# Two transformer blocks on one core: block 1's mixing stage put in another order, attention first, gates split around the state steps

## What is computed

```python
h = rms_norm(x, mix_norm)
p_rwkv, p_q, p_k, p_v, p_gate = split(h @ w_in)         # 3360, 768, 768, 768, 2048 columns
# branch a: RWKV-7
r, k, v, wd, ad, gd = split(p + (prev - p) * mu)        # prev: the token before
decay = exp(-exp(-softplus(-(w0 + tanh(wd) @ w2)) - 0.5)); a = sigmoid(a0 + ad @ a2); g = sigmoid(gd) @ g2
kk = k * k_k;  kk = kk / max(norm(kk over each head's 64), 1e-12)
k = k * (1 + (a - 1) * k_a)
wkv = scan over tokens of a 64x64 state for each of 16 heads
y_a = (groupnorm(wkv) * ln_w + ln_b + sum(r * k * r_k) * v) * g
# branch b: dilated attention, 3 groups of 4 heads (dilations 1, 4, 16), causal
q, k = rms_norm over each head's 64;  s = q k^T / 8 + mask;  softmax; o = p v
y_b = o * softmax over the 3 groups of each group's log-sum-exp
g_a, g_b = split(sigmoid(p_gate + b_gate))
x = x + (g_a * (y_a @ w_proj_rwkv) + g_b * (y_b @ w_proj_attn)) @ w_out
```

## Time and profile before

| | us |
|---|---|
| median of 3 runs | 3079.72 (3071.02 to 3081.1) |
| the profiled execution | 3080.11 |
| its span, first to last instruction | 3078.5 |
| PE busy | 2830.0 (92%) |
| DVE busy | 760.7 (25%) |
| ACT busy | 361.0 (12%) |
| the mixing stage of block 1 (PE's first product to its last) | 586.65 |

### The profile page before, as it was taken

The page is one execution under the profiler, slowest core; times in us unless marked ns, Lnnn a source line. Parts: engine busy times, 40 slices in busy tenths (PEclk is TensorE's granted clock), DMA queues, the critical chain, the costliest instruction groups (busy, mean ns, idle before and its releaser), DMA issues.

```text
span 3078.5 us, 70725 instructions
## 1 busy us (share of the span) xinstructions
PE 2830.0 (92%) x32566; PEld 2331.4 (76%) x32566; DVE 760.7 (25%) x1322; ACT 361.0 (12%) x807; POOL 9.4 (0%) x21
## 2 busy tenths in 40 slices
PE   7998968993989999998999899989999999999997
PEld 6776857872667766873776667747999999999995
DVE  0002247546177733332000233321000000000002
ACT  1001122213010012410000124101000000000000
POOL 0000000000000000000000000000000000000000
PEclk9999989896999999998999899989999999999999
DMA  4433320030333432332344323325999999999993
GB/s 189 163 151 150 125 96 3 4 111 21 123 124 147 164 147 89 137 137 100 123 163 165 139 96 117 129 100 212 375 398 369 376 403 371 377 391 373 377 387 124
DMA packets 54385, 596.12 MB, mean 194 GB/s; under 512 B 6128, under 2 KB 6512, under 8 KB 8672
## 3 DMA queue, kind: packets, MB, share of 16 engines
q1 hardware_dynamic: 52464, 587.71, 48.9%
q0 software_dynamic: 1776, 6.20, 0.6%
HBM read 592.83 MB, written 1.05 MB: 193 GB/s over the span
## 4 chain that ended last, share of the span: by engine, by line
PE 88%; DVE 6%; DMA 3%; ACT 1%; issue 1%; SPq 0%; DVEq 0%; ACTq 0%
PE bank L306 20%; PE bank L1994 18%; PE bank L397 15%; PE bank L2006 9%; PE bank L314 8%; PE bank L408 7%; DMA slot<-in_experts 2%; PE bank L791 2%; PE bank L2087 1%; PE bank L373 1%; PE bank L2039 1%; PE bank L1574 1%; DVE arena L1156 1%; PE bank L774 0%; PE bank L1462 0%
## 5 line engine op out<-in xcount | busy, mean ns | idle before, releaser
L1994 PE MATMUL bank<-arena,slot 128*64 128x96 f32 x14336 | 615.4, 246 | 8.1 <-issue 6.2
L1994 PEld LDWEIGHTS bank<-arena,slot 128*64 128x64 f32 x14336 | 601.3, 137 | 11.7 <-issue 11.3
L397 PE MATMUL bank<-h_cm,slot 128*128 128x256 f32 x2112 | 464.8, 381 | 3.9 <-DVE h_cm L349 2.8
L306 PE MATMUL bank<-h_cm,slot 128*128 128x256 f32 (+1 forms) x2064 | 456.2, 383 | 3.6 <-DVE h_cm L351 2.3
L397 PEld LDWEIGHTS bank<-h_cm,slot 128*128 128x128 f32 x2112 | 403.8, 191 | 72.5 <-issue 18.4
L306 PEld LDWEIGHTS bank<-h_cm,slot 128*128 128x128 f32 (+1 forms) x2064 | 394.2, 191 | 65.0 <-issue 9.7
L2006 PE MATMUL bank<-ff,slot 128*64 128x96 f32 x7168 | 319.9, 246 | 13.5 <-DMA slot<-in_experts 10.3
L2006 PEld LDWEIGHTS bank<-ff,slot 128*64 128x64 f32 x7168 | 306.3, 137 | 15.9 <-issue 15.0
L2154 DVE TENSOR_TENSOR ff<-ff,bank 128x192 f32<-128x192 f32 x112 | 39.7, 354 | 800.5 <-PE bank L1994 800.5
L408 PE MATMUL bank<-slot,ff 128*128 128x512 f32 x528 | 231.5, 592 | 0.0
L408 PEld LDWEIGHTS bank<-slot,ff 128*128 128x128 f32 x528 | 100.3, 190 | 113.5 <-issue 111.9
(11 more groups left out here) (358 smaller groups left out, 1678.0 us busy)
## 6 DMA issues: line engine op xcount, KB each, us to landing
slot<-in_experts SPq DMA_DIRECT2D x112, 2048.0 KB, 8.9
slot<-in_experts SPq DMA_DIRECT2D x112, 1024.0 KB, 9.2
slot<-in_ffn SPq DMA_DIRECT2D x22, 2048.0 KB, 9.1
slot<-in_ffn SPq DMA_DIRECT2D x22, 1024.0 KB, 4.9
slot<-in_dense SPq DMA_DIRECT2D x11, 2048.0 KB, 8.8
slot<-in_dqk SPq DMA_DIRECT2D x8, 2048.0 KB, 8.5
slot<-in_g SPq DMA_DIRECT2D x8, 2048.0 KB, 8.1
slot<-in_w_in_rkv SPq DMA_DIRECT2D x6, 2048.0 KB, 8.2
```

The source lines that it names most:

```text
L306: ins = pe.matmul(ps[0:m, j * S:(j + 1) * S], w[:, k * width + c0:k * width + c0 + m], rhs[:, k, :], start=k == 0, stop=k == ks - 1)
L397: ins = pe.matmul(bank[:, m * S:(m + 1) * S], slot[s][:, c0:c0 + P], h_cm[:, k, :], start=k == 0, stop=k == KD - 1)
L1994: ins = pe.matmul(bank[64 * c:64 * c + 64, m * PLACES:(m + 1) * PLACES], slot[s][:, c0:c0 + 64], QUEUE[:, e, k, :], start=k == 0, stop=k = ...
```

## The change

The stage's products are put in another order, and several small computations get another form:

1. PE begins with q and k (packed so that slab n holds the tiles of three products for each half `u` of the heads), then k of RWKV, and lays the steps of attention between the products of v, r, k and the small products (`pe_block1`, with `act_block1` and `dve_block1`).
2. Gate slabs 0 and 1 stand at the end of `pe_block1`, ahead of the chunks; slabs 2 and 3 stand between the state steps.
3. `head_sums` makes each head's sum into 32 rows of one bank (3 or 4 matmuls with 32 output columns in one bank), the root and the reciprocal are done there on 512 columns, and `head_spread` spreads the result with matmuls over 32 rows, one bank each. This replaces the wide form for `qks`, `kks` and `gnv`.
4. The softmax over the keys of all three groups of a head is done at once, with one maximum and one sum over the groups; the second softmax over the groups is gone.
5. The projection of y_b (`attn_branch`) stands beside the group norm's steps, and y_a and the merged sum are passed on in four parts (`y_a_ready`, `merged1`).
6. The small RWKV matrices are a slab of the stream in place of three loads at the start; at the start c_dilated (576 KB) is loaded in place of c_rwkv (320 KB), and POOL's queue loads c_rwkv when both halves' masks were used. c_always is 128 columns (64 KB) wider.

```diff
+        for name, n in (("w_in_a", 0), ("w_in_qk", 0), ("w_in_qk", 1), ("w_in_qk", 2), ("w_in_rkv", 2), ("w_in_rkv", 3),
+                        ("w_in_v0", 0), ("w_in_v1", 0), ("lora", 0), ("w_in_rkv", 0), ("w_in_rkv", 1), ("w_in_rkv", 4),
+                        ("w_in_rkv", 5), ("w_in_gates", 0), ("w_in_gates", 1), ("w_in_gates", 2), ("w_in_gates", 3),
+                        ("w_proj_attn", 0), ("w_proj_attn", 1), ("w_proj_rwkv", 0), ("w_proj_rwkv", 1), ("w_out", 0), ("w_out", 1)):
+            stream.append(((name, n), dram[name][n], dram[name].shape[2]))
...
+        def head_sums(pe, key, src, pairs):
+            ps = fill(pe, key, next_bank())
+            for q, n in enumerate(pairs):
+                ins = pe.matmul(ps[32 * q:32 * q + 32, :], headones[:, 48:80], src[:, n:n + 2, :], start=True, stop=True)
+            filled(ins, key)
+        def head_spread(pe, key, q, src):
+            rows = slice(32 * q, 32 * q + 32)
+            ps = fill(pe, key, next_bank())
+            filled(pe.matmul(ps[:, :], pick[rows, :], src[rows, :], start=True, stop=True), key)
...
+            for n in range(4):
+                qk(n)
+            qk_sums(0)
+            qk(4)
+            qk(5)
+            qk_sums(1)
+            rkv(2)
+            qk_spread(0)
+            rkv(3)
+            qk_spread(1)
+            scores(0)
+            product_tm(pe, ("va0", 0), next_bank(), w, 512, 0, 512, h_cm, KD, 0)
+            scores(1)
+            product_tm(pe, ("va0", 1), next_bank(), w, 512, 0, 512, h_cm, KD, 1)
...
+            head_sums(pe, ("kks", 0), TMP, range(0, 8, 2))
...
+            turned_probs(0)
+            lora("w", w)
...
+                head_spread(pe, ("kkb", b), b, KKI)
+            lora("a", w)
+            lora("g", w)
+            attn_out(0)
+            turned_probs(1)
+            rkv(0)
+            attn_out(1)
+            rkv(1)
+            rkv(4)
...
+            rkv(5)
+            pe_gate(pe, 0)
+            pe_gate(pe, 1)
...
+            states(1)
+            pe_gate(pe, 2)
+            states(2)
+            pe_gate(pe, 3)
+            states(3)
             pe.wait_ge(named("wkv_ready"), 1)
...
+            pe.wait_ge(named("centred_squared"), 4)
+            head_sums(pe, ("gnv", 0), CUM, range(0, 8, 2))
...
+            attn_branch(0)
+            pe.wait_ge(named("gn_inverse"), 1)
+            for b in range(4):
+                head_spread(pe, ("gnb", b), b, GNI)
+            attn_branch(1)
...
-            ch.step(nc.vector.reciprocal(CUM, CUM))
-            ch.step(nc.vector.tensor_tensor(TMP, TMP, CUM, ALU.mult))
-            ch.step(nc.vector.tensor_tensor(TMP, TMP, spread(col("ln_w", 0, 8), S), ALU.mult))
-            ch.step(nc.vector.tensor_tensor(TMP, TMP, spread(col("ln_b", 0, 8), S), ALU.add))
-            ch.step(nc.vector.tensor_tensor(TMP, TMP, BONUS, ALU.add))
-            nc.vector.tensor_tensor(K, TMP, G, ALU.mult).then_inc(named("y_a_ready"), 1)
...
-            pool.wait_ge(named("y_a_ready"), 1)
-            pool.dma_start(turn_consts[:, 0:3 * KEYS], dram["c_dilated"]).then_inc(named("masks_loaded"), 16)
+            pool.wait_ge(named("masks_used"), 1)
+            pool.dma_start(turn_consts[:, 0:CONSTANTS["rwkv"].shape[1]], dram["c_rwkv"]).then_inc(named("rwkv_consts"), 16)
...
-            sp.dma_start(arena[:, 20480:21504], dram["lora_wa"]).then_inc(named("lora_loaded"), 16)
-            sp.dma_start(arena[:, 18432:19456], dram["lora_g"]).then_inc(named("lora_loaded"), 16)
-            sp.dma_start(arena[0:32, 19456:20480], dram["lora_g2"]).then_inc(named("lora_loaded"), 16)
```

More of the change, by code:

```diff
@@ L120, in constants @@
     add("always", "headones", row // HD == col // HD)
+    add("always", "pick", row % 32 == 16 * (col // HD))
     half = 16
@@ new lines, in pe_block1 @@
+            lora("a", w)
+            lora("g", w)
+            released(("lora", 0), ("g", 3))
+            attn_out(0)
[4 more added lines that the diff above has]
+            rkv(4)
+            pe.wait_ge(named("rk_ready"), 1)
+            for b in range(4):
+                ps = fill(pe, ("bonus", b), next_bank())
+                filled(pe.matmul(ps[:, :], headones, TMP[:, 2 * b:2 * b + 2, :], start=True, stop=True), ("bonus", b))
+            rkv(5)
@@ new lines, in pe_block1, with act_gate, act_block1, keep_raw @@
+            pe_gate(pe, 0)
+            pe_gate(pe, 1)
+        def act_gate(act, tile):
+            dst = (gates_a, gates_b)[tile // 8]
+            ps = full(act, ("gate", tile))
+            for j in range(2):
+                ins = act.activation(dst[:, tile % 8 + j, :], ps[:, j * S:(j + 1) * S], ACT.Sigmoid,
+                                     bias=col("b_gate", tile + j))
+            free(ins, ("gate", tile))
+        def act_block1(act, ch):
+            def keep_raw(n):
+                key, parts = SHIFTS[n]
@@ L668, in act_rwkv_in @@
-            for tile in range(0, 16, 2):
-                if tile == 4:
-                    act_decays(act)
-                ps = full(act, ("gate", tile))
-                for j in range(2):
-                    ins = act.activation(gates[:, tile + j, :], ps[:, j * S:(j + 1) * S], ACT.Sigmoid,
-                                         bias=col("b_gate", tile + j))
-                free(ins, ("gate", tile))
-        def act_decays(act):
+                free(act.copy(raw[n % 2][0:m, 0:len(parts), 1:S + 1],
+                              ps[0:m, 0:len(parts) * S].rearrange("p (k s) -> p k s", s=S)), key)
@@ L693, in dve_rwkv_in, with dve_block1, shift @@
+            attn_out(0)
+            probs(1)
+            keep_raw(6)
+            keep_raw(7)
+            attn_out(1)
+            for n in range(8, 14):
+                keep_raw(n)
+            for tile in (0, 2, 4, 6):
+                act_gate(act, tile)
+        def dve_block1(dve, ch):
+            def shift(n):
+                key, parts = SHIFTS[n]
                 drained(dve, key)
@@ new lines, in turned_probs @@
+            def turned_probs(u):
+                for n in (1, 3):
+                    ps = full(dve, ("pt", u, n))
+                    free(nc.vector.tensor_copy(PT_FLAT[:, 512 * n:512 * n + 512], ps[:, :]), ("pt", u, n))
+            h_written(dve, ("norm", "mix"))
+            for i in range(2):
+                ch.add(nc.vector.memset(raw[i][:, :, 0:1], 0.0))
+            ch.fence()
+            dve.sem_inc(named("shift_zero"), 1)
+            shift(0)
+            shift(1)
+            qk_meansq(0)
@@ L867, in pe_rwkv_chunks, with states @@
                     drained(pe, ("QG", j, c))
[L868 removed]
+            def states(c):
                 pe.wait_ge(named("state_ready"), c)
```

677 lines of the change are left out of this document (355 added, 322 removed).

## The result

| | before | after |
|---|---|---|
| median, us | 3080.41 (3071.02 to 3084.22, 4 runs) | 2981.84 (2973.96 to 2984.4, 4 runs) |
| ratio after / before | | 0.968, 95% interval 0.9651 to 0.9709 |
| the profiled execution, its span | 3080.11, 3078.5 | 2980.48, 2978.7 |
| the mixing stage | 586.65 | 488.1 |
| from its end to the end of the program | 2228.2 | 2227.6 |

The forecast was 2982. The stage runs from 263.04 to 751.14 us. It gave 98.5 of the 99.8 us by which the span is shorter; the rest of the program before it and after it is 0.6 us shorter each.

What follows compares the result with a forecast made beforehand. The stage was taken as bound by the order of PE's work around DVE's chains. Terms 231.1 + 8.3 + 129.5 + 118.9 = 487.8 against 586.65, 98.9 less; 3080.1 - 98.9 + 1.0 = 2982.2, forecast 2982, 8-in-10 range 2968 to 3004.

Steps and rivals of the forecast that it cites:

- work in the block (with 2.0 for shape changes): Stage up to `tm`: products and small operations 225.8 us, plus 2.0 for some ten tile-shape changes at 0.2.
- Bound by the order of PE's work around DVE's chains: Mixing stage: PE stands still 107 of 586.65 us, nearly all behind DVE chains, while products needing none stand further down.
- a whole start: Tile-mode changes: if 0.9 us were lost at each of some twelve, the sum would be 9 us higher.
- Narrow matmuls side by side: `head_sums` and `head_spread`: neighbours overlap, 0.9 to 1.1 us per group; rival, one after another, 17 us more, chance 0.15.
- The 1.3 ahead of the second `qks`: In the block, PE waits 1.3 us for ACT's square of the last q/k product.
- the 1 us in hand ahead of the first spread: Half 0's `qk_inverse`, under the r/k/v product of 13.8 us, is done 1 us before PE wants it.
- The 2.0 us for the banks of g: Half 1's transpositions `pt` wait 2.0 us for g's four banks, which ACT reads only after its three exponentials.
- the 1.1 us for a bank behind y_a's parts: Behind the chunks, PE waits 1.1 us for a bank DVE frees after y_a's four parts, 10.6 us in all.
- the second rival: DVE or ACT late inside the new block: 2.5 us at each of five places, 12 us, 2994; chance 0.17.
- Gates between the state steps hide both waits: Behind the chunks, gate products of 27.6 us hide both waits between the three state steps.
- The reason for taking off 1.3 us: Chunks 130.8 us less about 1.3, since their first matmuls no longer follow a long stand: 129.5.
- The clock: Rival: lowered clock on 345 us of PE work outside the chunks takes part or all of the gain; chance 0.04.

Runs made afterwards that it cites:

- e4: Changed kernel with gate slab 1's two products in the first two turns of the chunk loop; median 2973.44 us, stage 490.2 us.
- e9: The kernel of e4 run once more with nothing edited; median 2969.97 us, stage 478.6 us.
- e2: Changed kernel with gate slabs 2 and 3 behind the third state step instead of between the steps; median 2978.46 us.
- e7: Kernel before, in its old order, with only kk, q and k given the narrow form (head_sums, head_spread); median 3047.46 us.
- e5: Changed kernel with every head_spread matmul reading the same rows 0 to 31 (wrong heads' factors); median 2994.68 us.
- e6: Changed kernel with the reciprocals of qk_inverse (both halves) and kk done three times instead of once; median 3000.22 us.

## Why the prediction was right

Term by term, in the changed kernel's first profile:

| term | predicted | measured |
|---|---|---|
| work in the block (with 2.0 for shape changes) | 227.8 | 227.2 busy |
| waits in the block | 3.3 | 1.6 |
| `tm` with its wait | 8.3 | 8.0 |
| chunks | 129.5 | 132.1; 129.5 in the second profile |
| behind the chunks | 118.9 | 119.2; 117.8 in the second |
| stage | 487.8 | 488.1; 483.9 in the second |
| x at the start | +1.0 | 0 |

- *Bound by the order of PE's work around DVE's chains.* Shown in the main: PE's idle time in the stage fell from 107 to 18 us, and the narrow form in the old order gives 32 of the 99 us. That the other 67 are nearly all the order's is argued from the waits: in the old order those of 20.4 and 8.2 us stand as they were, and of the first at most 4.4 us are the second softmax.
- *Prices.* 41.45 / 192 for a record and the walk through the order gave the block's work within 0.6 us. The 2.0 us for shape changes are in it and were not measured by themselves. The Trainium skill, TensorEngine Tiling (Tiling Modes), has a change of mode drain the array; the trace agrees that there is something to pay, and 0.9 us for each change, which would have been 9 us more, is ruled out. (The prediction called these 0.9 us a whole start; by its own rows they are one wide matmul with its start.) Of a spread with 32 rows between two projections nothing can be seen beyond its 1.07 us.
- *Narrow matmuls side by side.* Shown twice, by 1.06 us in the changed kernel and 2.77 us with the rows made equal.
- *The waits.* The 1.3 ahead of the second `qks`, 1.5 ahead of `gnv` and the 1 us in hand ahead of the first spread came out within 0.1. The 2.0 us for the banks of g did not come: ACT had read them in time. Nor did the 1.1 us for a bank behind y_a's parts: DVE's four parts took 9.8 us (685.32 to 695.1) where 10.6 were put, and were through before y_b's second half was. The longest wait is not where it was expected, ahead of the half-1 transpositions, but ahead of the first state step, 1.8 us for DVE, as before. DVE or ACT being late inside the block, the second rival, did not happen: apart from the 1.4 us ahead of the second `qks` no wait stands in the block at all but 0.2 us (L315).
- *Gates between the state steps hide both waits.* True, and worth 0.3 us. It was right to price the products, not the cover.
- *The chunks.* The reason for taking off 1.3 us (no long stand before them) was wrong: their first levels ran at half clock as before (a granted clock of 0.72 at 507 to 511 us). Their length is not fixed to better than 9 us: in six profiles in which nothing in them was edited they took 123.5 to 132.1 us, the longer the lower their clock (0.99 to 0.90).
- *The clock.* As a rival it was put too low. It was thought of as something that would take the whole gain, with 0.04; what exists is a loss of 8 to 15 us in the block, in 4 of 10 profiles of kernels with the new order. The changed kernel's nine executions (2967.9 to 2984.4) spread over 17 us. With a fall in the block like e4's its profile would have shown 7.5 us more, still inside the range.
- *How near it came is partly luck.* The mechanism held, but the stage within 0.3 us and the run within 0.2 us did not have to be: waits put 1.7 us too high and chunks put 2.6 us too low cancel, the 1.0 us for x was not there, and the same program's second profile is 4.2 us shorter.

## What to carry to other kernels

Where an engine waits for a long chain of another, look first for work that needs none of it and stands further down, and price the move by walking the new order with the old trace's prices; here that came within 0.3 us of the stage in one profile and within 4 us in another. Reduce per-head factors before roots and reciprocals, keep them on 32 rows, and put neighbours on different rows or columns of the array, so that three or four matmuls cost one. Before an edit is blamed or praised for less than 10 us, profile the same program twice and compare the granted clock window by window. Compare a stretch only with one of the same clock: four products in the chunks looked as if they cost 15.9 us, and cost 24.5.

## What the runs showed of the hardware

The granted clock of TensorE was 0.50 (1.2 GHz) for 14 to 31 us while it was busy, and for one program (e4 and e9) it was so in one execution and not in another. It is found in 4 of 10 profiles in the stretch of small tiles (64 and 32 rows, transpositions, 64 columns) from 387 to 431 us, and in e7 at 311 to 327 us. It rose again in every one of them, with the same work or with the wide products behind it. In e2, e4 and e7 it fell in the middle of g's pairs of 128 and 32 rows (a pair from then on takes 2.3 us in place of 1.25), in e5 and e6 6 to 7 us ahead of them; e7 has these pairs at another place of the program, and the profile of before passes them at 1.00. The Trainium skill, TensorE: Matmul & The Clock Gate (HAM oscillation), puts a loss of clock in the middle of a kernel down to gaps in which the engine is idle; the rows of e2, e4, e5 and e7 do not agree, as PE is busy in every microsecond of those stretches and of the 8 us before; in e6 alone a wait of 2.7 us stands at the beginning. Why it falls in one execution and not in another stays open: no run here tells a property of the small tiles from a phase that differs between executions. That it is at the small tiles in all five is an observation, not a cause shown.
